# Branch A's probabilities scaled by 1/sum on the scalar engine instead of the vector engine

## What is computed

```
m = jnp.max(s, axis=-1)
m = jnp.maximum(m, sk)                     # sk: the sink
p = jnp.exp(s - m[..., None])
denom = jnp.sum(p, axis=-1) + jnp.exp(sk - m)
o = jnp.einsum('nchgqk,nckhd->ncqhgd', p, vv.astype(jnp.float32))
o = o / denom_t[..., None]
```

## Time and profile before

| | us |
|---|---|
| median of 3 runs | 1379.47 |
| lowest, highest | 1378.44, 1379.62 |
| the profiled execution | 1380.62 |
| its span, first to last instruction | 1378.8 |

### The profile page before, as it was taken

How to read it: one execution, slowest core, us unless ns; L and a number is a source line. 1 busy time by engine, 2 the same in 40 slices (tenths; PEclk the granted TensorE clock), 3 DMA queues, 4 the chain that set the end, 5 groups by cost and what they waited for, 6 DMA issues and landing times.

```text
span 1378.8 us, 19889 instructions
## 1 busy us (share of the span) xinstructions
PE 1359.5 (99%) x6488; PEld 1153.5 (84%) x6488; DVE 479.4 (35%) x846; ACT 574.7 (42%) x971; POOL 671.2 (49%) x512
## 2 busy tenths in 40 slices
PE   9999999999999999999999999999999999999996
PEld 7888888888988988898898888888888888888884
DVE  4866665662030223204111011010101202287688
ACT  5465464543471374356247222222222222445442
POOL 4633443455455556546454555464555636422214
PEclk9999999999999999999999999999999999999998
DMA  8442241445374355337444344653536446377674
GB/s 258 132 127 77 76 137 49 134 115 126 91 167 144 81 115 141 124 86 167 145 111 141 89 151 117 144 139 101 171 94 159 123 127 146 98 246 259 202 253 154
DMA packets 204990, 190.07 MB, mean 138 GB/s; under 512 B 16528, under 2 KB 178576, under 8 KB 204944
## 3 DMA queue, kind: packets, MB, share of 16 engines
q1 hardware_dynamic: 191344, 151.74, 37.8%
q0 software_dynamic: 13600, 37.75, 11.3%
HBM read 185.23 MB, written 41.94 MB: 165 GB/s over the span
## 4 chain that ended last, share of the span: by engine, by line
PE 68%; issue 16%; POOL 11%; DMA 2%; DVE 1%; ACT 1%; POOLq 0%; SPq 0%; ACTq 0%
PE acc L1517 61%; POOL w_lo L577 6%; POOL w_lo L576 5%; PE ps_scores L1517 2%; DMA raw<-w_in 1%; PE ps_out L1517 1%; PE ps_turn L1517 1%; PE ps_out L1607 1%; DMA raw<-w_out 0%; PE ps_turn L1579 0%; DVE z L1375 0%; PE ps_scores L1544 0%; DMA raw<-xT 0%; PE ps_scores L1541 0%; DVE x_lo L983 0%
## 5 line engine op out<-in xcount | busy, mean ns | idle before, releaser
L576 POOL TENSOR_TENSOR w_lo<-raw,w_hi 128x512 fp32r<-128x512 f32 x242 | 322.7, 1334 | 689.9 <-ACT w_hi L630 567.9
L1517 PE MATMUL acc<-x_hi,w_hi 128*128 128x512 f32 x1216 | 477.9, 393 | 0.0
L1517 PE MATMUL acc<-x_hi,w_lo 128*128 128x512 f32 x1216 | 474.2, 390 | 0.0
L1517 PE MATMUL acc<-x_lo,w_hi 128*128 128x512 f32 x1216 | 474.0, 390 | 0.0
L630 ACT ACTIVATE w_hi<-raw 128x1024 fp32r<-128x1024 f32 x224 | 234.2, 1056 | 338.8 <-PE acc L1517 330.0
L577 POOL TENSOR_TENSOR w_lo<-raw,w_hi 128x512 fp32r<-128x512 f32 x242 | 333.7, 1379 | 0.0
L1517 PEld LDWEIGHTS acc<-x_hi,w_lo 128*128 128x128 f32 x1216 | 228.2, 188 | 48.0
L1517 PEld LDWEIGHTS acc<-x_hi,w_hi 128*128 128x128 f32 x1216 | 228.5, 188 | 44.3 <-POOL w_lo L577 0.2
L1517 PEld LDWEIGHTS acc<-x_lo,w_hi 128*128 128x128 f32 x1216 | 228.5, 188 | 44.1
L1240 DVE TENSOR_TENSOR part_a<-acc,part_a 128x512 f32<-128x512 f32 x16 | 11.1, 691 | 321.7 <-PE acc L1517 321.5
L1517 PE MATMUL acc<-w_hi,x_lo 128*128 128x384 f32 x256 | 85.6, 334 | 0.0
(11 more groups left out here) (275 smaller groups left out, 1605.4 us busy)
## 6 DMA issues: line engine op xcount, KB each, us to landing
raw<-w_in SPq DMA_DIRECT2D x384, 128.0 KB, 2.3
q_left<-w_out POOLq DMA_DIRECT2D x12, 2048.0 KB, 13.6
raw<-w_in SPq DMA_DIRECT2D x256, 96.0 KB, 2.6
raw<-q_left SPq DMA_DIRECT2D x32, 512.0 KB, 4.7
raw<-w_in SPq DMA_DIRECT2D x64, 192.0 KB, 3.0
raw<-w_pa SPq DMA_DIRECT2D x64, 128.0 KB, 6.1
raw<-w_out SPq DMA_DIRECT2D x16, 512.0 KB, 4.4
raw<-xT SPq DMA_DIRECT2D x8, 512.0 KB, 5.0
```

Of the source, the lines that this page charges most:

```text
L576: nc.gpsimd.tensor_tensor(dst[:, left], raw[:, slot, left], hi[:, left].bitcast(F32), ALU.subtract)
L1517: ins = nc.tensor.matmul(into[:, 0:cols], s, m, start=start and k == 0, stop=stop and k == n - 1)
```

## The change

ScalarE gets a new function, `divide_a`, which waits for the reciprocal and multiplies the two heads' probabilities in place by an activation of the kind Copy with a per-partition scale. It stands in ScalarE's program at the step normalise of `A_PLAN`. VectorE's `normalise` keeps the reciprocal and loses its own wait for it and the two multiplications. TensorE waits for the same semaphore (`normalised`), which ScalarE now raises.

```
+            def divide_a(u, a):
+                act.wait_ge(recip_ready, a + 1)
+                for hh in range(2):
+                    p = probs_a[:, u % 2, hh, (P if u % 4 == 0 else 0):2 * P]
+                    last = nc.scalar.activation(p, p, ACT.Copy, scale=rdenom[:, u % 2, hh:hh + 1])
+                last.then_inc(normalised, 1)
...
+                    if stage == "normalise":
+                        divide_a(u, first_unit + u)
                     if stage == "collect":
...
                 nc.vector.reciprocal(rdenom[:, j, 0:2], denom[:, j, 0:2]).then_inc(recip_ready, 1)
-                dve.wait_ge(recip_ready, a + 1)
-                for hh in range(2):
-                    p = probs_a[:, j, hh, (P if u % 4 == 0 else 0):2 * P]
-                    last = nc.vector.tensor_scalar(p, p, rdenom[:, j, hh:hh + 1], None, ALU.mult)
-                last.then_inc(normalised, 1)
```

## The result

The changed kernel takes 1381.34 us (median of 22 runs, 1379.51 to 1383.22) against 1379.78 us of the kernel before (22 runs, 1378.03 to 1381.23). The ratio is 1.0013, with an interval of 1.0007 to 1.0019: slower by 1.6 us by the medians, clear of zero and inside the 0.2% that the prediction called no change. The forecast was 1381.2, +0.12%.

A forecast was written before the change was run, and what follows sets the result against it. TensorE, busy 99% of the span, was taken to bound the kernel. Terms 0.4+0.28+0.79+0.23 gave +1.7 us, 1382.3 against the profiled execution, 1381.2 (+0.12%) after adjusting to the runs' median; range 1379.3 to 1383.6.

The forecast's parts named there:

- The sum: Whole kernel: 0.4 (passes 1 to 3) + 0.28 + 0.79 + 0.23 (pass 4) = +1.7 us, bounds 1.2 to 2.8.
- passes 1 to 3, units 0 and 1: Scaling 1 stands ahead of the copy of unit 0's transposes, delaying the probsT_lo product: +0.13 us each, 0.4 in three.
- unit 2 there: Passes 1 to 3: pair 0.28 us later against 0.30 room, mask rather earlier; taken as 0, upper bound 0.03 each.
- pass 4, unit 1: The stretched 2.25 us pair goes but the copy is late in its turn; product at 257.19 instead of 257.51: -0.32 us.
- pass 4, up to unit 2's values: Unit 2's scaling waits behind a conversion, transposes at 263.75 instead of 263.47; unit 1's gain lost, +0.28 us stands.
- unit 6: Pass 4: scaling stands behind two conversions, transposes at 286.64 instead of 285.85: +0.79 us.
- unit 7: Pass 4: scaling stands behind the swap of bank 1, transposes at 292.60, due at 292.37: +0.23 us.
- The durations: ScalarE scaling pairs: 256 wide takes 0.89 us; 128 wide holds the engine 0.60.
- The handoff: From VectorE's reciprocal to a waiting scalar engine: 0.04 us kept, at most 0.2, which would bring the sum to 2.8.
- The slower one: Rival: vector engine not relieved, scaling on TensorE's path in every early unit; 0.3 at nine places, +4.4 us, 1383.9; chance 0.21.
- The faster one: Rival: only the relief counts; at most the 1.0 us probsT_lo wait and about 0.1 in other passes, 1378.2; chance 0.04.
- the sentence that nothing later could absorb a stall: TensorE has no later gap (280.00 of 280 us busy in 420 to 700), so a branch A stall arrives whole.

The follow-up runs named there:

- Run 6: Kernel before, VectorE still scaling, plus an idle pair of scalar-engine copies at each place where the change scales, nothing waiting for them: 1380.11 us against 1379.70, ratio 1.0001.
- Run 4: Changed kernel with one edit, the copy of unit 0's transposes ahead of scaling 1: 1380.06 us, ratio 0.9999 to the kernel before.
- run 5: Changed kernel with a second pair of copies ahead of every scaling's pair: 1393.66 us, ratio 1.0103 to the kernel before.
- run 3: Changed kernel, all scaling on ScalarE, with copy, conversions and swap reordered around scalings at four places: 1378.28 us against 1379.60 before, ratio 0.9990.

## Why the prediction was right, point by point

**The sum.** Forecast +1.7, pass lengths +1.66, measured +1.56 by the medians (ratio 1.0007 to 1.0019, so 1.0 to 2.6 us). Part by part, in us:

| place | forecast | timeline after |
|---|---|---|
| passes 1 to 3, units 0 and 1 | +0.13 each | +0.07, +0.07, +0.10 at unit 1's transposes |
| unit 2 there | 0 | 0 |
| pass 4, unit 1 | -0.32 | -0.36 |
| pass 4, up to unit 2's values | +0.28 | +0.29 |
| unit 6 | +0.79 | +0.79 |
| unit 7 | +0.23 | +0.25 |

The -0.36 is contained in the +0.29, as in the forecast. What is left to +1.49, 0.16, comes in steps of 0.02 to 0.06, the largest right behind the first transpose of units 6 and 7. That sum and medians agree within 0.2 us is partly luck, since the interval alone is 1.6 us wide; that the parts agree is not.

**The first line** was too large, by about half in two of the three passes: the exponentials of unit 1 weren't later at all, and the first product on the copied transposes could already start where it had. In the timeline after, 0.14 us earlier in the span from the pass's start on:

```profile
83.93 0.49 ACT L637 ACTIVATE probs_a<-probs_a,negmax 128x257 f32<-128x257 f32 x1
...
85.24 0.91 ACT L645 ACTIVATE probs_a<-probs_a,rdenom 128x256 f32<-128x256 f32 x2 [0.23 <-DVE rdenom L1079]
86.06 0.36 ACT L701 ACTIVATE probsT_hi<-ps_turn 128x256 fp32r<-128x256 f32 x1
...
86.93 0.39 PE L1599 MATMUL ps_out<-probsT_lo,v_hi_a 128*128 128x256 f32 x1
```

**The durations** taken from branch B held: pairs of 0.89 to 0.91 us, and a 128 wide pair of 0.68 that holds the engine for 0.58 (in pass 4 from 253.00 to the exponentials at 253.58; I had taken 0.60). **The handoff** that had no row was 0.03: the reciprocal ends at 85.21 and the scaling starts at 85.24. At all 15 places where the scalar engine stood idle for the reciprocal it was 0.03. I had kept 0.04, and the upper bound of 0.2 was never near; the terms that I named for it add up to 0.14 (0.03 and 0.04, and as much again), not to 0.2. The formula of the Trainium skill (ScalarE: Activation LUTs, section "What ACT_TABLE_LOAD costs") gives, as an estimate, 387 ns for 128 wide and 493 for 256; the rows have 385 at least and 494 in the median.

**Unit 2** of passes 1 to 3 was the step with the thinnest slack, and I took 0 for it because the mask would come earlier. It did, by 0.77 us relative to the pass's start, and TensorE didn't wait. The mechanism was the one named: q_split took 0.69 us and not 1.69, GpSimd's subtraction starting after it. The kernel before, then the changed one:

```profile
86.86 1.28 POOL L576 TENSOR_TENSOR w_lo<-raw,w_hi 128x512 fp32r<-128x512 f32 x1 [0.65 <-ACT w_hi L630]
86.98 1.69 DVE L1181 TENSOR_TENSOR q_split<-q_a,q_split 64x512 fp32r<-64x512 f32 x1
...
86.91 0.69 DVE L1185 TENSOR_TENSOR q_split<-q_a,q_split 64x512 fp32r<-64x512 f32 x1
87.44 1.31 POOL L576 TENSOR_TENSOR w_lo<-raw,w_hi 128x512 fp32r<-128x512 f32 x1 [1.39 <-ACT w_hi L630]
```

Run 6 shows that the late conversion does this by itself. There the vector engine still multiplies, and q_split starts where it does in the kernel before (both 0.39 us earlier in the span). Only GpSimd is later:

```profile
86.59 0.69 DVE L1190 TENSOR_TENSOR q_split<-q_a,q_split 64x512 fp32r<-64x512 f32 x1
86.86 1.57 POOL L577 TENSOR_TENSOR w_lo<-raw,w_hi 128x512 fp32r<-128x512 f32 x1 [1.06 <-ACT w_hi L631]
```

**Pass 4, unit 2.** Right in size, and the reason was incomplete: I tied the vector engine's work there to GpSimd until 258.24. Run 4 shows that it is tied only as long as q_split comes second; with the copy 0.8 us earlier it isn't.

**The rivals.** The slower one (the pair on TensorE's path in every early unit) didn't happen; run 5 shows what it would have looked like. The faster one was bounded by the 1.0 us wait plus 0.1 in three passes, 1.3. The pass lengths of run 3 have 1.98 (1.3 by the medians): 0.24 to 0.28 in each loop pass, over twice what I allowed, and 1.22 in pass 4; still inside 0.2%.

**What was not right** is the sentence that nothing later could absorb a stall. I looked at 420 to 700 us and not at 300 to 420, where TensorE isn't busy throughout in the kernel before and the 1.4 us wait for probs_b ends with a load:

```profile
300.00:420.00 120.00, 118.62 (x600) 104.54 (x600) 29.21 (x49) 56.63 (x120) 67.69 (x52) 1.00 0.55 127
```

In the changed kernel's profile that wait is 1.0, and the one on more_lo, also behind a load, 0.5. TensorE's instructions are 1.53 us later at the end of pass 4, 1.18 behind the wait for probs_b and 0.6 at the end, so the profile's span grew by 0.6 us only. I had named a change in a later stage as a sign of being wrong, and by that sign this step was. The medians of 22 runs show 1.56, so for the forecast it made no difference that can be measured. Two smaller signs also came otherwise. The waits on probsT that I expected near 87, 143 and 200 us are not in the list of TensorE's waits; the 0.07 to 0.10 us show only in the starts. And the wait for the copy (probsT_hi, 0.4 us) in unit 1 of pass 4 I hadn't named, though my times for the copy contain it.

## What to carry to other kernels

When a step moves to another engine, list what stands ahead of it there and what it now stands ahead of, at each place apart, and compare each with the slack of whoever waits; the engine's idle share says nothing about it (23 us of load were free in run 6, and in pass 4 eight scalings, some behind conversions and one behind a swap, cost 1.5 us). If a move costs little or nothing, its order is worth a second look before it is given up: here edits of order at four kinds of places turned +0.13% into -0.10%. And look for idle time of the bottleneck in every later stage, not in the longest one, before you say that a stall arrives whole.

## What the runs showed that I had not expected

When a two-input operation of the vector engine and one of GpSimd meet on SBUF, the one that starts later is the one that is stretched, in the rows shown here. In the first pass q_split takes 1.69 us when it starts 0.12 us after GpSimd's subtraction, and 0.69 when it starts 0.27 us ahead of it, and then it is GpSimd's that takes 1.57 instead of 1.29. So a conversion on a third engine, 0.4 us later, moved the mask of another unit 0.8 us forward, with nothing changed on the vector engine.
